# Running gate sums of a gated delta layer: one product and a round trip through DRAM in place of sixteen broadcast products

## What is computed

```python
beta = jax.nn.sigmoid(b_logit)
g = -jnp.exp(a_log) * jax.nn.softplus(a + dt_bias)         # one gate per position and head
g_cum = jnp.cumsum(g, axis=-1)                             # running sums within a chunk
seg = g_cum[..., :, None] - g_cum[..., None, :]
decay = jnp.where(incl, jnp.exp(jnp.where(incl, seg, 0.0)), 0.0)
lower = jnp.where(strict, beta[..., :, None] * (k @ k^T) * decay, 0.0)
# (I + lower) is inverted; q k^T is also weighted with decay; the state is carried on
k_dec = k * jnp.exp(g_cum[..., -1:] - g_cum)[..., None]
```

## Time and profile before

| | |
|---|---|
| median of 3 runs | 2944.76 us (2943.22 to 2945.09) |
| span of the profiled execution | 2946.0 us |
| TensorE busy | 2891.8 us, 98% of the span |
| VectorE busy | 1813.9 us, 62% |
| ScalarE busy | 1598.2 us, 54% |
| GpSimd busy | 417.1 us, 14% |
| first gdn stage | about 193 to 394 us |
| second gdn stage | about 1697 to 1898 us |

### The profile page before, as it was taken

One profiled execution on the slowest core, in us unless ns is written; L12 is line 12 of the kernel. 1 busy time (PEld: TensorE's weight loads), 2 busy tenths in 40 slices (PEclk: granted clock), 3 DMA queues, 4 the chain that ended last, 5 costly groups with the idle time before them and its releaser, 6 DMA issues.

```text
span 2946.0 us, 36491 instructions
## 1 busy us (share of the span) xinstructions
PE 2891.8 (98%) x14543; PEld 2451.5 (83%) x14543; DVE 1813.9 (62%) x2192; ACT 1598.2 (54%) x2013; POOL 417.1 (14%) x636
## 2 busy tenths in 40 slices
PE   9999999999999999989999999999999999999998
PEld 7888888888988888878888888888888888888887
DVE  6568566555666556465556486555665765675664
ACT  5447754444464454565444377644565563566562
POOL 1203212021002112041202115021000020000020
PEclk9999999999999999999999999999999999999999
DMA  8754168676548677537768643376645596645694
GB/s 276 239 188 142 45 194 245 196 236 219 182 147 246 214 219 236 180 99 219 231 202 242 200 149 124 93 239 225 190 153 176 197 281 213 198 147 180 211 278 156
DMA packets 397050, 575.08 MB, mean 195 GB/s; under 512 B 20016, under 2 KB 248624, under 8 KB 396880
## 3 DMA queue, kind: packets, MB, share of 16 engines
q1 hardware_dynamic: 372624, 508.75, 54.9%
q0 software_dynamic: 23680, 62.95, 6.9%
q10 hardware_dynamic: 576, 1.05, 0.1%
HBM read 540.16 MB, written 32.51 MB: 194 GB/s over the span
## 4 chain that ended last, share of the span: by engine, by line
PE 85%; DVE 7%; ACT 5%; issue 1%; DMA 1%; POOL 0%; SPq 0%; DVEq 0%; ACTq 0%; POOLq 0%
PE ps L430 25%; PE ps L432 25%; PE ps L431 25%; PE ps L616 3%; DVE lo L656 2%; ACT hi L638 1%; DVE qkv L1641 1%; PE ps L503 1%; PE ps L505 1%; PE ps L504 1%; ACT sl L1416 1%; ACT qkv L1416 1%; PE ps L603 0%; PE ps L587 0%; DMA raw<-in_ffn_w_gu 0%
## 5 line engine op out<-in xcount | busy, mean ns | idle before, releaser
L656 DVE TENSOR_TENSOR lo<-raw,hi 128x2048 fp32r<-128x2048 f32 (+3 forms) x473 | 1057.5, 2246 | 654.0 <-ACT hi L638 653.4
L638 ACT ACTIVATE hi<-raw 128x2048 fp32r<-128x2048 f32 (+2 forms) x487 | 906.8, 1870 | 725.2 <-DMA raw<-in_ffn_w_gu 285.7
L430 PE MATMUL ps<-hi,xh 128*128 128x512 f32 (+1 forms) x2208 | 865.0, 392 | 5.5 <-DVE lo L656 2.3
L432 PE MATMUL ps<-hi,xl 128*128 128x512 f32 (+1 forms) x2208 | 858.0, 389 | 0.0
L431 PE MATMUL ps<-lo,xh 128*128 128x512 f32 (+1 forms) x2208 | 857.4, 388 | 0.0
L430 PEld LDWEIGHTS ps<-hi,xh 128*128 128x128 f32 x2208 | 414.6, 188 | 91.8 <-DVE lo L656 5.3
L432 PEld LDWEIGHTS ps<-hi,xl 128*128 128x128 f32 x2208 | 414.4, 188 | 86.1
L431 PEld LDWEIGHTS ps<-lo,xh 128*128 128x128 f32 x2208 | 414.8, 188 | 82.7
L430 PE MATMUL ps<-hi,hhh 128*128 128x512 f32 x704 | 274.6, 390 | 0.0
L432 PE MATMUL ps<-hi,hhl 128*128 128x512 f32 x704 | 274.0, 389 | 0.0
L431 PE MATMUL ps<-lo,hhh 128*128 128x512 f32 x704 | 273.9, 389 | 0.0
(11 more groups left out here) (443 smaller groups left out, 3405.0 us busy)
## 6 DMA issues: line engine op xcount, KB each, us to landing
raw<-in_ffn_w_gu SPq DMA_DIRECT2D x348, 512.0 KB, 4.8
raw<-in_ffn_w_down SPq DMA_DIRECT2D x80, 1024.0 KB, 5.3
raw<-in_w_ff SPq DMA_DIRECT2D x64, 1024.0 KB, 6.0
raw<-in_w_in SPq DMA_DIRECT2D x60, 1024.0 KB, 5.3
raw<-in_gdn_w_in SPq DMA_DIRECT2D x32, 1024.0 KB, 5.8
turned<-hhf POOLq DMA_DIRECT2D x88, 256.0 KB, 4.9
hhr<-turned POOLq DMA_DIRECT2D x352, 64.0 KB, 4.4
raw<-in_sb_w_in SPq DMA_DIRECT2D x12, 1024.0 KB, 5.1
```

The source lines that it names most:

```text
L430: e.matmul(o, a1, r1, start=kk == 0, stop=False)
L432: i = e.matmul(o, a2, r1, start=False, stop=kk == kts - 1)
L638: k.e.activation(k.m.hi[q % RING][:, 0:n], k.m.raw[q % RING][:, 0:n], ACT.Copy).then_inc(*k.up("act_piece_hi", ("hi", q)))
L656: k.e.tensor_tensor(m.lo[i][:, 0:n], m.raw[i][:, 0:n], m.hi[i][:, 0:n].bitcast(F32), ALU.subtract).then_inc(*k.up("dve_piece_lo", ("split" ...
```

## The change

One further product goes behind the small one in `gates`: the gates of all 16 pairs, padded with zeros to 128 columns (`gP`), times `C_UT`. It gives the 16 rows of running sums on 16 partitions. VectorE copies them to `gT` ahead of the copy to `GC`. GpSimd, in a new lane `gates`, sends `gT` (16 x 128, 8 KB) to DRAM, waits for that, and issues two reads that bring eight rows each to all 128 partitions, straight into the tile `qkD`, block 1 first. Each chain then waits for its block, subtracts `GC` with one operation of 128 x 512, and makes the two masked forms with two more. The four broadcast products of each chain, and their PSUM bank, go. `KE` for block 0 becomes a copy of column 127 of the exponentials that are there already. Only the script of GpSimd is altered; the scripts of the other engines are those of before.

```diff
+    gT, gP = kd[:, S:S + P], kd[:, S + P:S + 2 * P]
...
 GDN_POOL = """
-c2 c3 clear W W W W W W W W W W W W c2 W W c0 c0 c2 c0 W ...
+c2 c3 clear W W W W W W W W gates gates W W W W c2 W W c0 c0 c2 c0 W ...
...
 # tensor_gdn, gates
-        e.matmul(b.ps[:, 0:16], C(C_UT), r["G"].rearrange("p a b -> p (a b)"), start=True, stop=True).then_inc(*k.up("pe_four", ("gcum", g)))
+        G = r["G"].rearrange("p a b -> p (a b)")
+        e.matmul(b.ps[:, 0:16], C(C_UT), G, start=True, stop=True)
+        k.wait_ge("gz", g)
+        e.matmul(b.ps[:, P:2 * P], r["gP"], C(C_UT), start=True, stop=True).then_inc(*k.up("pe_four", ("gcum", g)))
 # tensor_gdn, chain
-        tensor_four(k, n("decay"), lambda h: r["G"][:, t, h0 + h:h0 + h + 1].to_broadcast([P, P]), lambda h: C(C_UT), ("g", g))
 # scalar_gdn, chain
         if t == 0:
-            k.wait_ge(*n("ke"))
-            act("act_chain", r["KE"][:, 1, h0:h0 + 4], r["KE"][:, 0, h0:h0 + 4], ACT.Exp, ("keD", g, g4))
+            k.wait_ge(*n("e2"))
+            act("act_chain", r["KE"][:, 1, h0:h0 + 4], r["qkD"][:, 4 * g4:4 * g4 + 4, 127], ACT.Copy, ("keD", g, g4))
 # vector_gdn, gates
         k.wait_ge("gcum", g)
+        e.tensor_copy(r["gT"][0:16, :], b.ps[0:16, P:2 * P]).then_inc(*up(("gT", g)))
 # vector_gdn, chain
-        b = k.bank(*n("decay"))
         k.wait_ge("gcum.s", g)
-        k.wait_ge(*n("decay"))
-        for h in range(4):
-            e.scalar_tensor_tensor(s[1][:, h, :], b.ps[:, h * P:(h + 1) * P], GC[...], C(C_NLE), ALU.subtract, ALU.subtract)
-        for h in range(4):
-            e.scalar_tensor_tensor(qkD[:, h, :], b.ps[:, h * P:(h + 1) * P], GC[...], C(C_NGT), ALU.subtract, ALU.add)
-        if t == 0:
-            e.tensor_tensor(KE[:, 0, h0:h0 + 4], q4(b)[:, :, 127], GC[:, 0, h0:h0 + 4], ALU.subtract)
+        k.wait_ge("gB", g, t)
+        e.tensor_tensor(qkD, qkD, GC[:, t, h0:h0 + 4].unsqueeze(2).to_broadcast([P, 4, P]), ALU.subtract).then_inc(*up(n("d")))
+        k.wait_ge(*n("d"))
+        e.tensor_tensor(s[1][:, :, :], qkD, C(C_NLE, 4), ALU.subtract).then_inc(*up(n("d1")))
+        e.tensor_tensor(qkD, qkD, C(C_NGT, 4), ALU.add).then_inc(*up(n("d2")))
 # pool_gdn
+        e.memset(r["gP"][:, 16:P], 0.0).then_inc(*k.up("pool_gdn", ("gz", g)))
+    def gates():
+        k.wait_ge("gT", g)
+        k.e.dma_start(k.t["gcum"], r["gT"][0:16, :]).then_inc(*k.up("dma_decay", ("gD", g), by=16))
+        yield
+        k.wait_ge("gD", g)
+        for t in (1, 0):
+            k.e.dma_start(r["qkD"][:, 8 * t:8 * t + 8, :], k.t["gcum"][8 * t:8 * t + 8, :].partition_broadcast(P)).then_inc(...("gB", g, t), by=16)
+        yield
```

More of the change, by code:

```diff
@@ L1221, in gdn_room @@
     sy = [m.tensor(f"sy{j}", [P, 4, P], F32, m.at_lrow + 2048 * j) for j in range(4)]
-    v = dict(qkv=qkv, zs=zs, vb=vb, kd=kd, qkD=qkD, baT=kd[:, 0:S], cin=cin, sq=[sy[0], sy[1], sy[3]],
+    v = dict(qkv=qkv, zs=zs, vb=vb, kd=kd, qkD=qkD, gT=gT, gP=gP, baT=kd[:, 0:S], cin=cin, sq=[sy[0], sy[1], sy[3]],
              slot={0: [sl[0], sl[1], sl[8], sl[9], sl[10]], 2: [sl[4], sl[5], sl[11], sl[12], sl[13]],
@@ L1231, in gdn_room @@
     for j, n in enumerate(("B", "G", "T1", "T2", "GC", "EG", "BE", "KE", "SS")):
-        v[n] = ga[:, 2 * j:2 * j + 2, :]
+        v[n] = ga[:, 2 * j:2 * j + 2, :] if n != "G" else gP[:, 0:16].rearrange("p (a b) -> p a b", a=2)
     return v
@@ L1254 @@
 GDN_POOL = """
-c2 c3 clear W W W W W W W W W W W W c2 W W c0 c0 c2 c0 W c1 c2 W c0 c3 c3 c3 c1 c1 W inv W c1 W W W W inv W W W c0 c3
-c2 c1 W W W c0 W c2 c0 W W c0 W c2 W c0 c3 W c1 c0 c2 c1 c3 c2 c3 c1 c2 c1 c0 c2 c3 c1 c1 c3 c3 W W W W W W W W
+c2 c3 clear W W W W W W W W gates gates W W W W c2 W W c0 c0 c2 c0 W c1 c2 W c0 c3 c3 c3 c1 c1 W inv W c1 W W W W inv
+W W W c0 c3 c2 c1 W W W c0 W c2 c0 W W c0 W c2 W c0 c3 W c1 c0 c2 c1 c3 c2 c3 c1 c2 c1 c0 c2 c3 c1 c1 c3 c3 W W W W W
+W W W
 """
@@ L1702, in chain @@
         yield
-        b = k.bank(*n("decay"))
         k.wait_ge("gcum.s", g)
-        k.wait_ge(*n("decay"))
-        for h in range(4):
-            e.scalar_tensor_tensor(s[1][:, h, :], b.ps[:, h * P:(h + 1) * P], GC[:, t, h0 + h:h0 + h + 1], C(C_NLE), ALU.subtract, ALU.subtract).then_inc(
-                *up(*([n("d1")] if h == 3 else [])))
-        for h in range(4):
-            e.scalar_tensor_tensor(qkD[:, h, :], b.ps[:, h * P:(h + 1) * P], GC[:, t, h0 + h:h0 + h + 1], C(C_NGT), ALU.subtract, ALU.add).then_inc(
-                *up(*([n("d2")] + ([b.read] if t else []) if h == 3 else [])))
-        if t == 0:
-            e.tensor_tensor(KE[:, 0, h0:h0 + 4], q4(b)[:, :, 127], GC[:, 0, h0:h0 + 4], ALU.subtract).then_inc(*up(n("ke"), b.read))
+        k.wait_ge("gB", g, t)
[3 more added lines that the diff above has]
+        e.tensor_tensor(qkD, qkD, C(C_NGT, 4), ALU.add).then_inc(*up(n("d2")))
         yield
@@ L1800, in clear @@
             k.wait_ge("used", plan.stage[g - 1][-1])
+        e.memset(r["gP"][:, 16:P], 0.0).then_inc(*k.up("pool_gdn", ("gz", g)))
         e.memset(r["Z"], 0.0).then_inc(*k.up("pool_gdn", ("z0", g)))
+        yield
[5 more added lines that the diff above has]
+        for t in (1, 0):
+            k.e.dma_start(r["qkD"][:, 8 * t:8 * t + 8, :], k.t["gcum"][8 * t:8 * t + 8, :].partition_broadcast(P)).then_inc(*k.up(f"dma_decays{t}", ("gB", g, t), by=16))
         yield
@@ L1837, in inv @@
         yield
-    run(script, {"W": pool_pieces(k, plan, g, ("conv", g, 22)), "clear": clear(), "c0": chain(0), "c1": chain(1), "c2": chain(2), "c3": chain(3), "inv": inv()})
+    run(script, {"W": pool_pieces(k, plan, g, ("conv", g, 22)), "clear": clear(), "gates": gates(), "c0": chain(0), "c1": chain(1), "c2": chain(2), "c3": chain(3), "inv": inv()})
 def sb_room(m):
@@ L3147, in program @@
         plan = Plan(t, [(si.name, si.i) for si in infos[:-1]], [si.late for si in infos])
-        t = dict(t, turned=nc.dram_tensor("turned", (4, P, 1024), F32, kind="Internal").ap())
+        t = dict(t, turned=nc.dram_tensor("turned", (4, P, 1024), F32, kind="Internal").ap(), gcum=nc.dram_tensor("gcum", (16, P), F32, kind="Internal").ap())
         c = Counts(nc, ctx, Mem(nc, ctx), t)
```

## The result

The changed kernel takes 2962.52 us in the median of 4 runs (2960.26 to 2963.54), beside 2944.47 us for the kernel before on the same chip: a ratio of 1.0061 (95% interval 1.0048 to 1.0074), some 18 us slower. The profiled run took 2962.93 us, with a span of 2961.1 us.

What follows compares the result with a forecast made beforehand. TensorE, busy 98%, was taken to have no slack against VectorE and ScalarE at k's third norm. Stalls less savings, 12.35 us, plus clock 1.0 us gave +13.4 us: 2958.0 us predicted, 0.45% slower, range 2951 to 2966 us.

Steps and rivals of the forecast that it cites:

- What bounds the place: From the first chain step on, VectorE and ScalarE end last; TensorE has no slack at k's third norm, 6 to 8 us idle expected.
- Rival 1: Round trip hidden behind TensorE's queue of split weight pieces; TensorE gains its 6.7 us, giving 2938 us; chance 5%.
- TensorE's 6.7 us counted at nothing: Chains' broadcast products removed, 7.1 us, less 0.44 us for the new product; none counted, since TensorE only reaches its waits earlier.
- The round trip: GpSimd's send to DRAM and read of block 1, in gates: 8.05 us, ends 6.0 and 10.8 us.
- The send: GpSimd's 8 KB send to DRAM: 2.85 us, the middle of 2.3 and 3.4 us.
- a sign of being wrong: Named signs: no new TensorE wait, send or read far off 2.85 and 4.8 us, or stage growth much below that wait.
- The read: Read of block 1, 512 KB, to all partitions: 4.8 us, at least 3.3 and at most 7.0 us.
- Taking up the signals: GpSimd and VectorE taking up their signals around the round trip: 0.1 us.
- The steps behind it: After block 1 lands: d1 at +1.4, second exponential +2.1, first tap +2.75, rounding +3.55 us; rounding 6.55 and 7.2 us late.
- The estimate of 5.6 us: Skill page's round trip, 2.0 us for the send plus 3.2 us for the read; whole sum near +8.5 us.
- VectorE's saving of 0.7 us a stage: Behind the first chain step, three 128 x 512 operations save 0.13 us for block 1, 0.2 to 0.35 us for block 0.
- The clock: TensorE's clock expected to fall to half after standing still some 7 us: 0.5 us a stage, ends 0 and 1.7.

Runs made afterwards that it cites:

- second experiment: Changed kernel with the 8 KB send made twice in series, each waited for, before the two reads: 2969.75 us, ratio 1.0091 to the kernel before.
- experiment without trip and masks: Changed kernel without send, its wait and reads, and without GpSimd's C_RO mask multiplications for chains c2 and c0: 2944.03 us, ratio 0.9999 to the kernel before.
- third experiment: Changed kernel with GpSimd's C_RO mask multiplication for chains c2 and c0 replaced by a one-element memset: 2960.73 us, ratio 1.0055 to the kernel before.
- the sixth: Changed kernel, c2's first step moved directly ahead of c0's, GpSimd masking c2 and c0 only after c1's subtractions: 2950.71 us, ratio 1.002 to the kernel before.
- fourth experiment: Changed kernel with c2's first step moved later on VectorE and ScalarE, directly ahead of c0's, nothing left out: 2950.01 us, ratio 1.0019 to the kernel before.

## Why the prediction was right, and where not

The forecast was 2958.0 us (+13.4 us), with a range of 2951 to 2966 us; the measured 2962.5 us (+18 us) lies within it, in its upper part. What makes the kernel slower, the wait for the trip that is handed on to TensorE, was foreseen. That the time stayed in the range is in part luck: the largest miss, below, is of a term that the range did not allow for. By the steps of the prediction:

**What bounds the place: right.** TensorE has no slack at the third norm of k. Its wait there went from 0 and 0.84 us to 7.56 and 10.17 us, and the first stage grew with it one for one when the trip was lengthened (second experiment; in the second stage VectorE's wait and the stage grew alike, and TensorE came later to its own wait). The wait of 10.17 us is above the 6 to 8 us that were named. Rival 1, a hidden trip, is out.

**TensorE's 6.7 us counted at nothing: right.** The experiment without trip and masks is the measurement of it: 0.9999 (0.9989 to 1.0008), where 6.7 us would be 0.23%. TensorE's busy time fell by 5.1 us only, though 6.7 us of products went; its product of the third norm ran at half clock (below), which adds to it.

**The round trip: 8.05 us forecast, 8.36 and 9.87 us measured.** The sum came near, but its parts did not, and they erred in opposite directions; that they made up for each other is luck. The send was put at 2.85 us with going on at 0.3 (3.15 together), and took 1.91 us in the first stage and 4.93 in the second: the middle of 2.3 and 3.4 us is a value that it never has in these runs. A send or read far off 2.85 and 4.8 us was named as a sign of being wrong, and for the send it came. The read was put at 4.8 us and took 6.16 and 4.64. Taking up the signals was put at 0.1 us, and GpSimd alone needs 0.3 us from the end of the copy. The steps behind it hold: the rounding is 6.83 us late in the first stage (242.72 - 235.16, less the 0.73 us with which the stage began) against 6.55, and 8.97 us in the second against 7.2. That term was too small by 2.05 us in all.

The estimate of 5.6 us from the page "DMA: Bandwidth & Descriptors" of the Trainium skill, section "Anatomy of one DMA", was too low: the trip was 8.4 and 9.9 us. Of its parts, the fixed 2.0 us lies between the quick send, which lands after 1.62 us, and the slow one with 4.65 us, and the read took 6.07 and 4.55 us to land where the estimate has 3.2.

**VectorE's saving of 0.7 us a stage: wrong, and the largest error.** The step of `c0` came out 0.44 us shorter, its wait included, but 0.22 us of that were spent waiting for ScalarE's first tap behind it (0.80 us idle in place of 0.58); the table has the rest (7.56 to 7.33). The added copy cost what was forecast: it holds the next one up by 0.2 us. But for `c3` I took the price of three operations from rows with an idle GpSimd. I read of the operands only their size, and not that the two inputs now both come from SBUF where one had come from PSUM. So 0.13 us won became 1.9 us lost, in both stages. The shift behind `c0` was to fall by some 0.5 us a stage and rose by 2.07: 5.1 us in all. Of this the contention makes 1.8 us a stage, 3.6 us: the third experiment takes it away, and in the sixth it moves to the taps. The other 0.8 us a stage, 1.5 us in all, are a saving that does not come even without the masks, for there the shift still rises by 0.27 us: VectorE is quicker with `c1`, but then waits longer for the first tap (in the third experiment 1.19 us where it was 0.82), since ScalarE sets the pace there. The contention stood in plain view in the trace of before, on a line that I did not look for. VectorE in the kernel before, with GpSimd beside it:

```profile
304.70 4.13 DVE L1679 TENSOR_TENSOR qkv<-qkv,sy 128x512 f32<-128x512 f32 x1
```

```profile
303.67 14.61 POOL L676 TENSOR_TENSOR lo<-raw,hi 128x2048 fp32r<-128x2048 f32 x3 [17.39 <-DVE qkv L1641]
```

One such product takes 4.13 us here, where two take 1.30 us in the earlier trace rows.

**The clock: a fall in both stages, as forecast, and no price.** Windows of the kernel after (length, busy PE, PEld, DVE, ACT, POOL, granted clock, DMA share, GB/s):

```profile
250.00:251.00 1.00, 1.00 (x7) 1.00 (x7) 0.86 (x2) 0.99 (x2) 0.00 (x0) 0.50 0.00 0
251.00:252.00 1.00, 1.00 (x7) 1.00 (x7) 0.34 (x1) 0.98 (x3) 0.00 (x0) 0.69 0.00 0
...
1762.00:1764.00 2.00, 2.00 (x12) 2.00 (x12) 1.31 (x3) 1.97 (x6) 0.00 (x0) 0.57 0.00 0
```

TensorE's timeline there, first and second stage:

```profile
246.51 2.05 PE L1339 MATMUL ps<-sy,const 128*128 128x512 f32 x2 [7.56 <-ACT sy L1420]
248.48 3.52 PE L616 MATMUL ps<-qkv 128*128 128x128 f32 x16
...
1758.96 2.05 PE L1339 MATMUL ps<-sy,const 128*128 128x512 f32 x2 [10.17 <-ACT sy L1420]
```

After 7.56 us of standing still the clock is at the 1.2 GHz level until about 251.6 us, and the third norm takes 2.05 us where it took 1.12. But the shift of VectorE's splits does not rise from 7.56 over this stretch, it falls to 7.33. ScalarE does wait 0.22 and 0.87 us for the slowed norms, and its next rounding comes 8.32 us later than before (254.15 against 245.83), but VectorE has work until 256.71 and does not notice. For TensorE the wait for `qn` behind it falls from 1.7 to 1.1 us, so it takes up the rest. The 1.0 us that I put down for the clock was not spent.

**The sum.** Forecast stages 6.35 and 7.0 us (with the clock), 13.35 together; measured 8.7 and 10.8, together 19.5. The 6.1 us between them are the trip (+2.05), the contention (+3.6), the saving that did not come (+1.5), and the clock (-1.0). The medians say 18.05 us; that the stages say 1.5 us more, with one execution each, I leave at that, since single executions differ by 3 us.

**The parts as the runs price them.** By the ratios to the kernel before, the trip makes 0.55% or some 16 us (1.0061 against 1.0006), and the contention at `c3` what lies between 1.0006 and 0.9999, some 2 us, with intervals that overlap; by the stages it is 3.7 us. Of the orders tried none beats the kernel before; the best form with the real data is the fourth experiment, at 1.0019. Not tried were the send and the reads on another engine's queue, and a copy to all partitions without the way through DRAM.

## What to carry to other kernels

A transfer that replaces a short product is not priced by its bytes but by its place: ask which instruction of an in-order engine waits for it, what is queued behind that, and whether the work of the busiest engine hangs on that queue; and put the wait where the data are due, not where the product stood. When an operation is moved from PSUM to SBUF sources, look up what GpSimd does at that very time, and look in the trace of before for the same operation beside a busy GpSimd. Work taken from the engine that is busy 98% of the time is worth nothing ahead of a place where it waits for another.

## What was not expected of the hardware

- A send of 8 KB of GpSimd's queue is either quick or slow. Its landing in the kernel after:

```profile
DMA to landing us min/median/max: 1.6/3.1/4.6
```

and in the kernel with two sends the first of both stages:

```profile
DMA to landing us min/median/max: 1.6/1.6/1.6
```

The 1.6 us is below the shortest send of the kernel before, 2.3 us; the second send of the kernel with two sends takes 4.4 us in both stages. Over all profiled executions with the round trip, seven sends landed after 1.60 to 1.64 us and seven after 4.35 to 5.16. Behind a quick send the read of block 1 took 5.9 to 6.8 us, behind a slow one 4.0 to 4.6 us. In the kernel after, the DMA engines' share was 0.00 around the quick send (230 to 232 us) and 0.75 around the slow one (1742 to 1744 us), where a load of the weight ring had begun. The times fit a load that slows whichever transfer it meets, but that this is the cause was not tested.
- Two reads of 512 KB that broadcast 4 KB to each partition land in 4.5 to 6.8 us in the kernel after, within the 3.3 to 8.0 us of the sends of the same size.
- VectorE's 128 x 512 operation with two inputs in SBUF goes from 0.69 to 1.64 and 1.79 us beside a GpSimd multiplication, GpSimd's own from 1.29 to 3.49 us, and six taps beside the masks from 2.47 to 4.57 us. An operation that took its rows from PSUM was not slowed beside the same multiplication (1.12 us for four, in the kernel before).
